# Splitting the stationary and the moving reads of a float32r matmul stream by 16-byte lines

## What is computed

```python
for i in range(2):
    if i == 0:
        h = h + stick_breaking_mixer(rmsnorm(h, sb_norm), w_qkv, w_o)   # 2048 -> 6144, 2048 -> 2048
    else:
        h = h + chunked_gmlp_mixer(rmsnorm(h, gm_norm), w_in, v_norm, w_s, b_s, w_o)  # 2048 -> 4096, 2048 -> 2048
    gate, up = jnp.split(rmsnorm(h, ffn_norm[i]) @ w_gate_up[i], 2, axis=-1)          # 2048 -> 11264
    h = h + (jax.nn.silu(gate) * up) @ w_down[i]                                      # 5632 -> 2048
return rmsnorm(h, final_norm)
```

## Time and profile before

| what | value |
|---|---|
| median of 3 runs (lowest, highest) | 2097.83 us (2097.77, 2097.84) |
| span of the profiled execution | 2097.8 us |
| time of the profiled execution itself | 2097.8 us: the runs and the span differ by under 0.1 us |
| TensorE matmuls busy | 2088.2 us, 9281 instructions |
| VectorE busy | 1430.7 us |
| ScalarE busy | 1013.1 us |
| mean granted clock of TensorE, share of full speed | 0.999 |
| DMA | 402.47 MB, mean 192 GB/s |

### The profile page before, as it was taken

One profiled execution on the slowest core, in us unless ns is written; L12 is line 12 of the kernel. 1 busy time (PEld: TensorE's weight loads), 2 busy tenths in 40 slices (PEclk: granted clock), 3 DMA queues, 4 the chain that ended last, 5 costly groups with the idle time before them and its releaser, 6 DMA issues.

```text
span 2097.8 us, 27159 instructions
## 1 busy us (share of the span) xinstructions
PE 2088.2 (100%) x9281; PEld 1729.4 (82%) x9281; DVE 1430.7 (68%) x1822; ACT 1013.1 (48%) x1285; POOL 16.4 (1%) x30
## 2 busy tenths in 40 slices
PE   9999999999999999999999999999999999999998
PEld 7888888888888888888888888888888888888887
DVE  6787777867666676665557887877666676664444
ACT  6577765544444444444445444554444444444443
POOL 1000000000000000000000000000000000000000
PEclk9999999999999999999999999999999999999999
DMA  8555554666666666555566665566666666655554
GB/s 264 179 179 170 181 189 167 198 196 192 191 190 198 191 193 195 192 191 196 194 192 209 190 200 183 190 190 201 192 189 198 192 193 194 190 194 198 192 191 150
DMA packets 207419, 402.47 MB, mean 192 GB/s; under 512 B 12336, under 2 KB 13056, under 8 KB 206976
## 3 DMA queue, kind: packets, MB, share of 16 engines
q1 hardware_dynamic: 206496, 398.11, 61.1%
q0 software_dynamic: 688, 3.18, 0.4%
q10 hardware_dynamic: 176, 0.40, 0.1%
HBM read 399.55 MB, written 2.10 MB: 191 GB/s over the span
## 4 chain that ended last, share of the span: by engine, by line
PE 99%; issue 0%; DMA 0%; DVE 0%; ACT 0%; POOLq 0%; POOL 0%; DVEq 0%; SPq 0%
PE acc L1085 64%; PE acc L1091 32%; PE tp L1156 0%; PE tp L1176 0%; PE acc L1106 0%; PE acc L1107 0%; PE acc L1108 0%; PE tp L1302 0%; DMA h<-in_x 0%; PE tp L1116 0%; PE acc L1345 0%; PE acc L1344 0%; PE acc L1343 0%; PE acc L1143 0%; PE tp L1136 0%
## 5 line engine op out<-in xcount | busy, mean ns | idle before, releaser
L654 DVE TENSOR_TENSOR w_lo<-raw,w_hi 128x1024 fp32r<-128x1024 f32 x750 | 916.0, 1224 | 584.9 <-ACT w_hi L348 581.1
L348 ACT ACTIVATE w_hi<-raw 128x1024 fp32r<-128x1024 f32 x750 | 792.9, 1060 | 922.4 <-PE acc L1091 917.2
L1085 PE MATMUL acc<-w_hi,xT 128*128 128x512 f32 x4032 | 998.7, 390 | 0.0
L1085 PEld LDWEIGHTS acc<-w_hi,xT 128*128 128x128 f32 x4032 | 756.0, 188 | 155.9
L1091 PE MATMUL acc<-w_lo,xT 128*128 128x512 f32 x2016 | 539.2, 389 | 0.0
L1091 PEld LDWEIGHTS acc<-w_lo,xT 128*128 128x128 f32 x2016 | 378.6, 188 | 78.5
L1085 PE MATMUL acc<-w_hi,hid_hi 128*128 128x512 f32 x944 | 368.7, 391 | 0.0
L1085 PE MATMUL acc<-w_hi,hid_lo 128*128 128x512 f32 x944 | 367.6, 389 | 0.0
L1091 PE MATMUL acc<-w_lo,hid_hi 128*128 128x512 f32 x944 | 252.5, 389 | 0.0
L1091 PEld LDWEIGHTS acc<-w_lo,hid_hi 128*128 128x128 f32 x944 | 177.3, 188 | 36.7
L1085 PEld LDWEIGHTS acc<-w_hi,hid_hi 128*128 128x128 f32 x944 | 177.3, 188 | 36.8
(11 more groups left out here) (115 smaller groups left out, 477.6 us busy)
## 6 DMA issues: line engine op xcount, KB each, us to landing
raw<-in_ffn_w_gate_up SPq DMA_DIRECT2D x352, 512.0 KB, 4.5
raw<-in_ffn_w_down SPq DMA_DIRECT2D x176, 512.0 KB, 3.6
raw<-in_sb_w_qkv SPq DMA_DIRECT2D x95, 512.0 KB, 4.3
raw<-in_gm_w_in SPq DMA_DIRECT2D x64, 512.0 KB, 4.4
raw<-in_sb_w_o SPq DMA_DIRECT2D x32, 512.0 KB, 4.1
raw<-in_gm_w_o SPq DMA_DIRECT2D x32, 512.0 KB, 4.0
h<-in_x SPq DMA_DIRECT2D x3, 512.0 KB, 7.6
gain_bc<-in_gm_v_norm POOLq DMA_DIRECT2D x1, 1024.0 KB, 6.1
```

What stands on the lines that cost most here:

```text
L348: nc.scalar.activation(w_hi[:, p % RING], raw[:, p % RING], ACT.Copy).then_inc(hi_ready, 1)
L654: nc.vector.tensor_tensor(w_lo[:, p % RING], raw[:, p % RING], w_hi[:, p % RING].bitcast(f32), ALU.subtract).then_inc(lo_ready, 1)
L1085: nc.tensor.matmul(acc_at(chunk, r), part[:, kt, rs], w_hi[:, p % RING, k], start=(kt == 0 and part is hi), stop=False)
```

## The change

- `xT` and `hid` get a new layout. Tiles stand in groups of four. Within a group the order is token, then part (low, high), then tile: 4 floats (16 bytes, `LINE` = 4) of the low parts of four tiles for a token, then 4 floats of the high parts. A stationary operand so takes 128 floats that are 32 bytes apart. Low parts lie in even 16-byte lines and high parts in odd ones.
- Each matmul takes its 512 weight columns as the 64 even lines of 4 columns and then the 64 odd ones, and writes the result columns to their old places (`by_lines` on the moving operand and on the output).
- `w_lo` starts 16 bytes later.
- The products of a tile and row tile are issued together, low by `w_hi` first, then high by `w_hi`, then high by `w_lo`. TensorE waits for `hi_ready` and `lo_ready` before the first of a piece.
- The engines that write the parts write single floats 32 bytes apart (one tile) or 4 floats 32 bytes apart (four tiles at once, read from PSUM tile by tile for each token).
- The scratch tensors that share the region move with it. Their sizes and the number of matmuls stay.

```diff
-        xT = sb("xT", [P, KD, 2, S], f32r)
-        xT_hi, xT_lo = xT[:, :, 0], xT[:, :, 1]
+        HI, LO = 1, 0
+        xT = sb("xT", [P, KD // LINE, S, 2, LINE], f32r)
+        xT_hi, xT_lo = xT[:, :, :, HI], xT[:, :, :, LO]
...
-        w_lo = sb("w_lo", [P, RING, KP, CH], f32r)
+        lows = sb("lows", [P, LINE + RING * KP * CH], f32r)
+        w_lo = lows[:, LINE:].rearrange("p (s k n) -> p s k n", s=RING, k=KP)
...
-        hid_hi = at("hid_hi", 0, [P, KF, S], f32r)
-        hid_lo = at("hid_lo", HB, [P, KF, S], f32r)
+        hid = at("hid", 0, [P, KF // LINE, S, 2, LINE], f32r)
+        hid_hi, hid_lo = hid[:, :, :, HI], hid[:, :, :, LO]
...
+        def lanes(t, group):
+
+            return t[:, bass.ds(group, 1)].rearrange("p g t k -> p (g t) k")
+
+        def lane(t, group, k):
+
+            return t[:, bass.ds(group, 1), :, k].rearrange("p g t -> p (g t)")
...
-                nc.scalar.activation(hid_hi[:, bass.ds(i * TC, TC), :],
-                                     tp[1][:, :].rearrange("p (k t) -> p k t", k=TC), ACT.Copy).then_inc(f_hi[layer], 1)
+                nc.scalar.activation(lanes(hid_hi, i),
+                                     tp[1][:, :].rearrange("p (k t) -> p t k", k=TC), ACT.Copy).then_inc(f_hi[layer], 1)
...
+            def by_lines(columns):
+
+                return columns.rearrange("p (c h e) -> p h c e", h=2, e=LINE)
+
+            def product(dst, part, kt, r, weight, start, stop):
+
+                return nc.tensor.matmul(by_lines(dst), part[:, kt // LINE, r * P:(r + 1) * P, kt % LINE], by_lines(weight), start=start, stop=stop)
+
...
-                    for k in range(KP):
-                        kt = k0 + k
-                        for r in range(RT):
-                            rs = slice(r * P, (r + 1) * P)
-                            for part in (hi, lo):
-                                nc.tensor.matmul(acc_at(chunk, r), part[:, kt, rs], w_hi[:, p % RING, k],
-                                                 start=(kt == 0 and part is hi), stop=False)
                     pe.wait_ge(lo_ready, base + it * per + p + 1)
...
-                        nc.tensor.matmul(dst, hi[:, kt, rs], w_hi[:, p % RING, k], start=(kt == 0), stop=False)
-                        nc.tensor.matmul(dst, hi[:, kt, rs], w_lo[:, p % RING, k], start=False, stop=False)
-                        last = nc.tensor.matmul(dst, lo[:, kt, rs], w_hi[:, p % RING, k], start=False,
-                                                stop=(kt == K - 1))
+                        product(dst, lo, kt, r, w_hi[:, p % RING, k], kt == 0, False)
+                        product(dst, hi, kt, r, w_hi[:, p % RING, k], False, False)
+                        last = product(dst, hi, kt, r, w_lo[:, p % RING, k], False, kt == K - 1)
                 last.then_inc(used, 1)
```

More of the change, by code:

```diff
@@ L357, in turned_gained @@
                 for k in range(TC):
-                    last = nc.scalar.activation(tile(xT_hi, c * TC + k),
+                    last = nc.scalar.activation(lane(xT_hi, c, k),
                                                 tp[0 if m or half(c) == 0 else 1][:, k * S:(k + 1) * S], ACT.Copy,
@@ L365, in x_tiles_gained @@
                 for k in ks:
[L366 removed]
+                    nc.scalar.activation(lane(xT_hi, k // TC, k % TC), tp[half(k // TC)][:, (k % TC) * S:(k % TC + 1) * S], ACT.Copy,
                                          scale=cols[:, k:k + 1]).then_inc(n_hi[0], 1)
@@ L664, in gained_low @@
                     last = nc.vector.scalar_tensor_tensor(
-                        out=tile(xT_lo, c * TC + k), in0=tp[0 if m or half(c) == 0 else 1][:, k * S:(k + 1) * S],
-                        scalar=cols[:, bass.ds(c * TC + (m * KD + k), 1)], in1=tile(xT_hi, c * TC + k).bitcast(f32),
+                        out=lane(xT_lo, c, k), in0=tp[0 if m or half(c) == 0 else 1][:, k * S:(k + 1) * S],
+                        scalar=cols[:, bass.ds(c * TC + (m * KD + k), 1)], in1=lane(xT_hi, c, k).bitcast(f32),
                         op0=ALU.mult, op1=ALU.subtract)
@@ L1075, in piece @@
                     pe.wait_ge(half_lo, p + 1)
-                elif first:
-                    pe.wait_ge(lo_ready, base + it * per + p + 1)
                 else:
                     pe.wait_ge(hi_ready, base + it * per + p + 1)
-                    for k in range(KP):
-                        kt = k0 + k
-                        for r in range(RT):
-                            rs = slice(r * P, (r + 1) * P)
-                            for part in (hi, lo):
-                                nc.tensor.matmul(acc_at(chunk, r), part[:, kt, rs], w_hi[:, p % RING, k],
-                                                 start=(kt == 0 and part is hi), stop=False)
-                    pe.wait_ge(lo_ready, base + it * per + p + 1)
-                    for k in range(KP):
-                        kt = k0 + k
-                        for r in range(RT):
-                            last = nc.tensor.matmul(acc_at(chunk, r), hi[:, kt, r * P:(r + 1) * P],
-                                                    w_lo[:, p % RING, k], start=False, stop=(kt == K - 1))
-                    last.then_inc(used, 1)
-                    return
+                    pe.wait_ge(lo_ready, base + it * per + p + 1)
                 for k in range(KP):
@@ L1342, in _ @@
                         kt = (t - PF) * KP + k
-                        nc.tensor.matmul(dst, hid_hi[:, kt, rs], w_hi[:, t % RING, k], start=False, stop=False)
-                        nc.tensor.matmul(dst, hid_hi[:, kt, rs], w_lo[:, t % RING, k], start=False, stop=False)
-                        last = nc.tensor.matmul(dst, hid_lo[:, kt, rs], w_hi[:, t % RING, k], start=False,
-                                                stop=(kt == KF - 1))
+                        product(dst, hid_lo, kt, r, w_hi[:, t % RING, k], False, False)
+                        product(dst, hid_hi, kt, r, w_hi[:, t % RING, k], False, False)
+                        last = product(dst, hid_hi, kt, r, w_lo[:, t % RING, k], False, kt == KF - 1)
                     if r == RT - 1:
```

41 lines of the change are left out of this document (19 added, 22 removed).

## The result

The kernel after takes 2260.35 us (median of 4 runs, 2260.28 to 2260.88), the kernel before 2097.84 beside it: a ratio of 1.0775 [1.076, 1.0791]. It is 162.5 us slower, 18.0 ns for each of the 9024 matmuls, and above the end of the range. The profiled execution took 2260.28 us; its span is 2258.5. The table ahead of the prediction gives 2097.8 us both for the profiled execution of the kernel before and for its span.

A forecast was written before the change was run, and what follows sets the result against it. TensorE, busy all the time with 9024 float32r matmuls at 226.7 ns, was taken as the bound. 2097.8 - 100.2 (excess gone) + 3 (wait for `w_lo`) + 1 (strided writes) = 2001.6, so 2002 us; 8-in-10 range 1994 to 2206.

The forecast's parts named there:

- The stationary operand 32 bytes apart: Stationary load touching 128 lines instead of 32: at most 227 ns at the moving operand's line rate; no term in the sum.
- Rival 1: Strided load spills into the matmul's second half and meets the moving operand's reads: +102 us, some 2204 us; chance 28%.
- Its worse form: Load's record of 188 ns grows by 107 and must end before the next matmul: 298 ns between starts, 2740 us.
- Separate lines: SBUF supposed to serve even and odd 16-byte lines apart; keeping both operand reads on different sides gains 100.2 us.
- the excess: 11.1 ns of each float32r matmul above a floor of 215.6 ns, supposed to be the two operand reads meeting.
- rival 2: Load and moving operand reads don't meet; the excess is the moving port's own at full rate: 2099 us; chance 12%.
- The price of 0.35 ns for each line of the load: The 11.1 ns of each matmul divided over the 32 lines that a contiguous stationary load reads.
- The result's columns in another order: Matmul output still written in runs of 16 bytes: nothing taken, bounded by 0 and 45 ns a matmul.
- The wait for `w_lo`: TensorE's wait at the head of a piece, 1.8 us earlier, hidden except in attention rounds: 3 us taken, at most 6.
- The strided writes: ScalarE and VectorE writing the parts; only the first eight tiles lie on the path: 0 to 4 us, 1 taken.
- the far end: Upper bound for strided writes, twice the streaming: +0.21 and +0.27 us for one tile, +0.85 and +1.07 for four.
- DMA: Scratch layout and transfers: same sizes and loads, 202 GB/s wanted, four ring slots for a load to land in; nothing.

## Why the prediction was wrong

**The step that failed** is "*The stationary operand 32 bytes apart*". The sum has no term for it: that the load's reading would fit in the first half of a matmul was the author's estimate, and no run shows it. What the traces show of contiguous loads is records of 188 to 192 ns and, at the position mixing, starts 0.111 us apart. A load of 128 floats 32 bytes apart takes about 240 ns: the same with 256 and with 128 columns moving. It does not fit beside a matmul that took 226.6 ns with contiguous loads, so it sets the pace. The line rate of the moving operand that the prediction gave, 1.77 ns a line, just missed the 1.87. It costs 13.6 ns a matmul: 2221.73 - 2097.84 - 1.1 = 122.8 us over 9024. How many floats a load takes from a line shows in the rows: records of 194 ns with two floats on a line, 308 and 331 with one.

**Rival 1** had the mechanism, a load that reads for over 107 ns, and its signs: records of 250 to 295 ns (331 in fact) and a pace of 238 or more (244). Its price of 2204 was too low, since it let the load fill only the matmul's 213 ns and priced meetings, while the load itself became the longest thing. Its worse form, in which the record's growth comes on top (2740 us), did not happen: records of 331 ns stand 244 apart and overlap.

**"*Separate lines*"** failed too, as a supposition. It gave 100.2 us of gain, and none came. Two things of it held: the excess comes with the reading of the moving operand (216.7 ns with one moving column, within 1.1 ns of the floor of 215.6), and the two reads do meet (226.8 or 233 by their distance alone), against rival 2. That the 11 ns at distance 0 are such meetings, and not the moving operand's own reading, is not shown; that half of rival 2 stays open. The price of 0.35 ns for each line of the load is refuted by the load of one float, and that only even and odd decide is refuted by the distances. A full separation of the parities, in the kernel with the strided loads and the weights apart, brought no gain to speak of: 238 ns against the load's 240. The measures it led to are themselves losses. Reading columns by lines costs 50 us with contiguous loads, and nothing in total beside strided ones. The shift of `w_lo` costs 38.6 us.

The prediction read the first matmuls, 0.427 us apart, as the lower level of the clock. That was inferred from the distance alone: the profile gives a granted clock of 1.00 there. The kernel with a quarter of the columns bears it out, with matmuls of 512 columns 427 ns apart (median) at a mean granted clock of 0.57.

**The sum as measured**: 2097.8 + 1.1 (order and waits) + 122.8 (strided load) + 38.6 (shift) = 2260.3. The terms add up because each is the difference between two kernels of a chain. The columns by lines and the strided writers with their waits are in the second term; that the former cost nothing beside strided loads was seen only with the shift in place.

**What held.** The result's columns in another order: nothing. The wait for `w_lo`: 3 us taken, 1.1 measured with the order, inside the noise. The strided writes: 1 us taken; the wait at the first tiles is 1.4 us, 0.6 more than with contiguous writes in the same order, with +0.24 and +0.21 us for a single tile (the far end said +0.21 and +0.27). In the kernel before ScalarE's writes from PSUM took 381 ns for 256 columns and 1026 for 1024 (L432, L539), 0.84 ns a column, and VectorE's 393 and 1218 (L763, L862), 1.07, so 256 columns more are 0.215 and 0.275 us. For four tiles, written in runs of 4 floats, the far end of twice the streaming was far off: they grew by 2 and 1 ns. DMA: nothing.

That the two reads don't meet at all, as in rival 2, does not agree with these runs: the pace hangs on what the moving side reads and on its distance to the load, 216.7 to 233.6 ns.

**Open.** Why the distance acts as it does; five pairs of distances give no rule. Three paces come back in kernels of different kinds: 226.7, 233.3 and 240.0 ns. At 2.4 columns a ns, the estimate from the 427 ns, they are 544, 560 and 576 columns, so 32, 48 and 64 over the 512; no run explains it. Why with the shift the products lose 4 ns on top of 240, when the load already bounds them: without it they are 240.6, 240.0 and 239.4 ns apart, with it 240.8, 245.9 and 246.7, so the second and third lose it. How the 4.2 ns of the 8-byte layout divide between 64 lines in the load and the shift of `w_lo` in that kernel. A separation with loads that read four floats a line and every other line was not tried.

## What to carry to other kernels

Before a stationary operand is laid out anew, count its floats on a 16-byte line. Here with two or four the load hid under a 512-column matmul (records of 194 and 188 ns). With one, 32 bytes apart, it took 240 ns and became the bound, which shows as PEld at 99% and records of over 300 ns; 16 bytes apart the records were over 300 ns too. The busy share of the loads, 82% before and 99% after, pointed at the cause, which the pace of 244 ns alone does not. And where a float32r stream stands a few per cent above its columns, look at the distance between the two operands' addresses: here a bad one cost up to 3% of the pace (233.6 against 226.7 ns) with no instruction changed. None of those tried was better than the one that the kernel had.

## What was not expected of the hardware

- A load at one float a line, 32 bytes apart, takes 240 ns in the mean at a granted clock of 1.00 and of 0.50 alike (256 and 128 columns moving).
- A stream that waits for its loads, 128 columns in 240 ns, shows TensorE busy 100% in the profile and yet a granted clock of 0.57; with 256 columns in 240 ns it stayed at 1.00.
- A load that reads one float 128 times is worse than one that reads 128 in a row: 2134.18 against 2098.98 us, one execution against eight.
- 512 columns read as every other line cost the moving side 5.5 ns with contiguous loads, and a shift of the addresses by 32 bytes costs 6.7.
